# Issue counts in a front stage's plan, and the fourth rotation placed behind the memory's low parts

## The reference

```python
x = x + 0.5 * rms_norm(swiglu(rms_norm(x, g1), w_gate, w_up, w_down), g1_post)
h = rms_norm(x, mix_pre_g)
proj = h @ w_in                      # columns for attention and for the recurrence
o_nsa = nsa_mixer(q, k_cmp, v_cmp, k_slc, v_slc, k_win, v_win, gate_logits, ...)
o_rwkv = rwkv7_mixer(r, k, v, w_lo, a_lo, g_lo, ...)
x = x + rms_norm(concat([rms_norm(o_nsa), o_rwkv]) @ w_out)
x = x + rms_norm(memory_cross_attention(rms_norm(x), rms_norm(mem), wq, wk, wv, wo))
x = x + 0.5 * rms_norm(swiglu(rms_norm(x, g2), w_gate, w_up, w_down), g2_post)
```

## Time and profile before

| | |
|---|---|
| median of 3 runs | 2557.35 us (2555.98 to 2559.16) |
| the profiled execution | 2554.12 us, span 2552.3 us |
| TensorE busy | 2488.6 us, 98% of the span |
| TensorE in the stretches 1020 to 1030 and 1030 to 1040 | 9.01 and 8.64 of 10 us |
| end of the last product of the front stage, about | 1077.5 us |
| first instruction of the next stage | 1081.55 us |

### The profile page before, as it was taken

One profiled execution on the slowest core, in us unless ns is written; L12 is line 12 of the kernel. 1 busy time (PEld: TensorE's weight loads), 2 busy tenths in 40 slices (PEclk: granted clock), 3 DMA queues, 4 the chain that ended last, 5 costly groups with the idle time before them and its releaser, 6 DMA issues. The chain is left out here.

```text
span 2552.3 us, 47185 instructions
## 1 busy us (share of the span) xinstructions
PE 2488.6 (98%) x19392; PEld 2038.3 (80%) x19392; DVE 1711.0 (67%) x2707; ACT 1054.6 (41%) x1824; POOL 95.3 (4%) x146
## 2 busy tenths in 40 slices
PE   8999999999899999899999998999999999999998
PEld 7788888888787778877888886877777888888887
DVE  6876676687555354488878888534457866766676
ACT  4322323344533343456555565523343322323443
POOL 0000000000000000011231110000000000000000
PEclk9999999999999999989999999999999999999999
DMA  4323324655332268832212115411121423225464
GB/s 150 99 82 119 123 71 142 219 196 158 96 122 93 62 205 239 235 98 58 50 43 49 41 45 205 143 58 34 66 75 61 135 97 119 98 91 209 142 197 145
DMA packets 279269, 297.92 MB, mean 117 GB/s; under 512 B 75442, under 2 KB 209840, under 8 KB 279088
## 3 DMA queue, kind: packets, MB, share of 16 engines
q1 hardware_dynamic: 276208, 292.59, 36.1%
q10 hardware_dynamic: 2880, 2.75, 0.4%
HBM read 208.67 MB, written 81.36 MB: 114 GB/s over the span
## 5 line engine op out<-in xcount | busy, mean ns | idle before, releaser
L1141 PE MATMUL f_ps<-hi,f_wh 128*128 128x512 f32 x672 | 261.9, 390 | 4.1 <-DVE f_wl L847 4.1
L1143 PE MATMUL f_ps<-hi,f_wl 128*128 128x512 f32 x672 | 261.5, 389 | 0.0
L2630 PE MATMUL f_ps<-hi,f_ahead_h 128*128 128x512 f32 x392 | 163.2, 416 | 0.8 <-PEq L72 0.8
L2632 PE MATMUL f_ps<-hi,f_ahead_l 128*128 128x512 f32 x392 | 153.1, 390 | 0.0
L2631 PE MATMUL f_ps<-one_lo,f_ahead_h 128*128 128x512 f32 x392 | 152.9, 390 | 0.0
L1141 PE MATMUL f_ps<-f_t3h,f_t2h 128*128 128x512 f32 x392 | 152.5, 389 | 0.0
L1142 PE MATMUL f_ps<-f_t3l,f_t2h 128*128 128x512 f32 x392 | 152.5, 389 | 0.0
L1143 PE MATMUL f_ps<-f_t3h,f_t2l 128*128 128x512 f32 x392 | 152.5, 389 | 0.0
L1141 PEld LDWEIGHTS f_ps<-hi,f_wh 128*128 128x128 f32 x672 | 126.1, 188 | 31.4 <-DVE f_wl L847 4.9
L1143 PEld LDWEIGHTS f_ps<-hi,f_wl 128*128 128x128 f32 x672 | 126.1, 188 | 26.3
L1142 PE MATMUL f_ps<-one_lo,f_wh 128*128 128x512 f32 x352 | 137.0, 389 | 0.0
(11 more groups left out here) (592 smaller groups left out, 6602.0 us busy)
## 6 DMA issues: line engine op xcount, KB each, us to landing
act<-one_y SPq DMA_DIRECT2D x30, 512.0 KB, 3.5
f_work<-act SPq DMA_DIRECT2D x30, 512.0 KB, 3.6
act<-y SPq DMA_DIRECT2D x30, 512.0 KB, 3.5
arena<-act SPq DMA_DIRECT2D x30, 512.0 KB, 3.6
one_y<-in_w_in SPq DMA_DIRECT2D x25, 512.0 KB, 4.5
early<-in_ffn_w_gate SPq DMA_DIRECT2D x11, 1024.0 KB, 6.4
early<-in_ffn_w_up SPq DMA_DIRECT2D x11, 1024.0 KB, 8.9
f_raw<-in_ffn_w_gate SPq DMA_DIRECT2D x10, 1024.0 KB, 6.2
```

The source lines that it names most:

```text
L1141: nc.tensor.matmul(out, wh, xh, start=start, stop=False)
L1143: return nc.tensor.matmul(out, wl, xh, start=False, stop=stop)
L2630: nc.tensor.matmul(dense_ps[:, b, cols], w_hi[:, b, k, :], hi[:, k, cols], start=(k == 0), stop=False)
L2632: mm = nc.tensor.matmul(dense_ps[:, b, cols], w_lo[:, b, k, :], hi[:, k, cols], start=False, stop=(k == KD - 1))
```

## The change

It adds a constant `ISSUE`, 0.61 us for each transfer that SyncE issues, and uses it in the planned time of each of SyncE's events, multiplied by the number of transfers. It also gives rotation 3 (the fourth, counted from 0) a further need: the low part `mlo` 1 of the memory. No instruction is added or taken away; only the order can differ. The diff, cut to the lines that differ:

```diff
 HOP = 0.2
+ISSUE = 0.61
...
-        event(("load", c), "sp", 0.5, *free, c and ("load", c - 1))
+        event(("load", c), "sp", ISSUE * (1 + {1: 13, 3: 10, PROJECTED - 2: 11, PROJECTED: 11}.get(c, 0)), *free, c and ("load", c - 1))
...
-                event(("store_vm",), "sp", 0.2, ("vcopy", 1), late=4.0)
+                event(("store_vm",), "sp", ISSUE, ("vcopy", 1), late=4.0)
...
-        event(("store_ops", p), "sp", 0.6, ("res", p), late=6.0)
-        event(("store_gate", p), "sp", 0.2, ("gr", p, 1), late=4.0)
+        event(("store_ops", p), "sp", 4 * ISSUE, ("res", p), late=4.0)
+        event(("store_gate", p), "sp", ISSUE, ("gr", p, 1), late=4.0)
...
-        event(("store_bonus", p), "sp", 0.2, ("bfin", p), late=4.0)
+        event(("store_bonus", p), "sp", ISSUE, ("bfin", p), late=4.0)
...
-            event(("store_v", n), "sp", 0.2, ("tcopy", n), late=4.0)
-    event(("load_mem",), "sp", 0.5, ("store_ops", 3), ("store_bonus", 3), late=16.0)
+            event(("store_v", n), "sp", ISSUE, ("tcopy", n), late=4.0)
+    event(("load_mem",), "sp", 3 * ISSUE, ("store_ops", 3), ("store_bonus", 3), late=16.0)
...
-    event(("load_w1", 0), "sp", 0.2, ("load", 3), late=7.0)
-    event(("load_w1", 1), "sp", 0.2, ("hid", 0), late=14.0)
+    event(("load_w1", 0), "sp", ISSUE, ("load", 3), late=7.0)
+    event(("load_w1", 1), "sp", ISSUE, ("hid", 0), late=14.0)
...
-        event(("spread", s), "sp", 0.5, ("evac", MIXED + s), ...
+        event(("spread", s), "sp", 4 * ISSUE, ("evac", MIXED + s), ...
...
-        event(("store_c", s), "sp", 0.3, ("cfin", s), late=3.0)
-    event(("tables",), "sp", 0.3, ("res", 3), late=5.0)
+        event(("store_c", s), "sp", ISSUE * (2 - s), ("cfin", s), late=3.0)
+    event(("tables",), "sp", 2 * ISSUE, ("res", 3), late=5.0)
...
-        event(("swap", n), "sp", 0.5, ("evac", at[("rot", n)]), ...
-        event(("rot", n), "dve", 3.8, ("swap", n), ("tables",), n and ("rot", n - 1))
+        event(("swap", n), "sp", 4 * ISSUE, ("evac", at[("rot", n)]), ...
+        event(("rot", n), "dve", 3.8, ("swap", n), ("tables",), n and ("rot", n - 1), n == 3 and ("mlo", 1))
...
-        event(("store_rot", n), "sp", 0.3, ("rlo", n), late=5.0)
+        event(("store_rot", n), "sp", 2 * ISSUE, ("rlo", n), late=5.0)
```

More of the change, by code:

```diff
@@ L2316, in front_plan @@
         event(("mlo", t), "dve", 1.4, ("mhi", t), t and ("mlo", 0))
-    event(("load_w1", 0), "sp", 0.2, ("load", 3), late=7.0)
-    event(("load_w1", 1), "sp", 0.2, ("hid", 0), late=14.0)
+    event(("load_w1", 0), "sp", ISSUE, ("load", 3), late=7.0)
+    event(("load_w1", 1), "sp", ISSUE, ("hid", 0), late=14.0)
     for s in range(2):
-        event(("spread", s), "sp", 0.5, ("evac", MIXED + s), ("gather", 0) if s else ("store_ops", 2), s == 0 and ("res", 2), late=4.5)
+        event(("spread", s), "sp", 4 * ISSUE, ("evac", MIXED + s), ("gather", 0) if s else ("store_ops", 2), s == 0 and ("res", 2), late=4.5)
         event(("gather", s), "dve", 2.6, ("spread", s), *([("hid", 0)] if s else [("zw", 3), ("rate", 3, 1), ("g", 3, 1)]))
@@ L2325, in front_plan @@
         event(("cfin", s), "dve", 0.3 if s else 1.2, ("cout", s), s and ("cfin", 0))
-        event(("store_c", s), "sp", 0.3, ("cfin", s), late=3.0)
-    event(("tables",), "sp", 0.3, ("res", 3), late=5.0)
+        event(("store_c", s), "sp", ISSUE * (2 - s), ("cfin", s), late=3.0)
+    event(("tables",), "sp", 2 * ISSUE, ("res", 3), late=5.0)
     for n in range(6):
-        event(("swap", n), "sp", 0.5, ("evac", at[("rot", n)]), *([("rot", n - 2)] if n >= 2 else [("store_ops", 3), ("bsum", 3, 1)]), late=4.0)
-        event(("rot", n), "dve", 3.8, ("swap", n), ("tables",), n and ("rot", n - 1))
+        event(("swap", n), "sp", 4 * ISSUE, ("evac", at[("rot", n)]), *([("rot", n - 2)] if n >= 2 else [("store_ops", 3), ("bsum", 3, 1)]), late=4.0)
+        event(("rot", n), "dve", 3.8, ("swap", n), ("tables",), n and ("rot", n - 1), n == 3 and ("mlo", 1))
         event(("rhi", n), "act", 1.2, ("rot", n), n and ("rhi", n - 1), *([("store_rot", n - 2)] if n >= 2 else [("store_ops", 3), ("cum", 3, 1)]))
         event(("rlo", n), "dve", 1.3, ("rhi", n), *([("store_rot", n - 2)] if n >= 2 else [("bfin", 3), ("store_gate", 3)]))
-        event(("store_rot", n), "sp", 0.3, ("rlo", n), late=5.0)
+        event(("store_rot", n), "sp", 2 * ISSUE, ("rlo", n), late=5.0)
     return in_order(engine, takes, needs, lag)
```

## The result

The changed kernel takes 2562.99 us in the median of 20 runs (2558.52 to 2571.25), the one before 2556.88 us on the same chips (20 runs, 2554.51 to 2564.28). The ratio is 1.0023, with an interval of 1.0015 to 1.0030: 5.9 us slower, between 3.8 and 7.7. That is inside the range of the prediction, and just past the bound that parts "no difference" from "slower".

The account below looks back on a forecast made before the run. The prediction took TensorE, 98% busy, as the bound, with SyncE's chain from rotation 5 ending the front stage. Rotation 5's late stores delay SyncE's 30.6 us of issuing: plus 4.0 us, median 2561.4, range 2554.5 to 2565.5.

Parts of the forecast that it names:

- Order on VectorE behind slab 25: VectorE, late front stage: rotations 3 to 5 follow the memory's low parts, interleaved with splits; `rlo` 5 ends 4.4 us late.
- The counts cost nothing: Front stage ahead of 1020: new issue counts delay memory loads behind slab 23; cost nothing, at most 2 us.
- TensorE by itself 0.6 us late: TensorE, late front stage: 1.0 us wait won, new 1.8 us wait, 1.2 us replacing 1.4; net 0.6 us late.
- 1 us of wait more for slab 35: TensorE near the stage's end: slab 35 lands 4.0 us later, is wanted 0.6 later, against 2.4 us of slack.
- The store of rotation 5: SyncE's queue: rotation 5's second store is issued at 1045.3 instead of 1040.89.
- Landing: Rotation 5's second store, behind a bunch of transfers, takes 8.2 us to land, at 1053.5 against 1049.5.
- 30.6 us of pure issuing: SyncE from slab 35 to the stage's end: never idle, so the list keeps its length and ends 4.0 us later.
- From the stage's end to the total: Next stage: can't give lateness back, so a stage ending 4.0 us later makes the total 4.0 us longer.
- rival 3: Rotations pile up: ScalarE waits for rotation 3's stores, `rlo` 5 slips another 2.88 us; plus 6.9 us, 2564.3; chance 0.34.
- land alone: Rival: rotation 5's stores land in 3.6 us, SyncE restarts early; minus 0.6 to plus 0.5 us, 2557; chance 0.12.
- The win: Rival: TensorE loses both waits (2.4 us), SyncE's chain no later; 4 us won at most, 2553.4; chance 0.06.

Follow-up runs that it names:

- the counts alone: Changed kernel without rotation 3's need for the memory's low part 1, so only the issue counts differ from before: 2558.44 us, ratio 1.0002.
- the run with the need on rotation 4: Kernel before, with rotation 4 instead of rotation 3 made to need the memory's low part 1: 2557.77 us, ratio 1.0002.
- the two held kernels: Kernel before, with slab 35 also waiting for the low part of slab 33, or of slab 34: 2562.16 us and 2563.26 us.
- The repaired kernels: Changed kernel, slabs 35 and 36 released by rotations 4 and 5, later slabs by their own buffer's stores; timed twice: 2559.16 and 2560.25 us.
- transfers taken early in the changed kernel: Changed kernel, with the next stage's two operand groups "across" issued ahead of slab 35: 2559.74 us, ratio 1.0007.
- the need alone: Kernel before, with only rotation 3's need for the memory's low part 1 added: 2562.15 us, ratio 1.0023.
- before's order with the transfers taken early: Kernel before, with the next stage's two operand groups "across" issued ahead of slab 35: 2557.22 us, ratio 1.0002.

## Why the prediction was right, and where it was off

The sum was plus 4.0 us, and the largest chance (0.59) went to a change within the 5.1 us that can be told; it is slower by 5.9 us, a little more than that, for which the chance was 0.36. The mechanism is in the main the forecast one, the lateness of rotation 5 carried through two stores into SyncE's list. That a late slab 35 alone costs that much was shown by holding it; that it is all of the loss was not. By its steps:

- *Order on VectorE behind slab 25*: each of the thirteen places as worked out. `rlo` 5 was to be 4.4 us late, it is 4.3.
- *The counts cost nothing*: right in its result (ratio 1.0002), short in its reason. The loads of the memory do go behind slab 23 and its leads, as worked out, and rotation 2 is no later for it (it starts 37.0 us ahead of T0, before 36.4). But the plan also changes ahead of 1020 on ScalarE and VectorE, where I found nothing: the counts move some early activations ahead of high parts of weights, and `rot` 2 and a low part ahead of a normalization. TensorE is busy for all of 700 to 1000 in both kernels, and that covers it. By the plan, the counts alone also put rotation 4 behind the low parts; the run with the need on rotation 4 shows that this costs nothing that can be told.
- *TensorE by itself 0.6 us late* (1.0 won, waits of 1.8 and 1.2), and 1 us of wait more for slab 35: the waits for low parts are 1.5 and 0.9, together 2.4 as before, and that behind slab 35 is 0.3. ScalarE's last transfer is 0.8 us later against T0. It stays off the path, as forecast.
- *The store of rotation 5*: issued 24.9 us after T0, where the profile before had 19.35. That is 5.5 us late, and the forecast had 4.4. The missing 1.1 us is issuing itself: in the bunch the load ahead of it took 0.85 us and the first store 1.63, where a lone store takes 0.34 to 0.43. I had given the bunch a price for landing and none for issuing.
- *Landing*: 8.2 us forecast, 7.3 measured. The two errors, 1.1 us too little for issuing and 0.9 too much for landing, all but cancel, and slab 35 is 4.2 us late where 4.0 was said. That this term came out so close was luck. The size that the Trainium skill (DMA: Bandwidth & Descriptors, the section Anatomy of one DMA) would give, an estimated 3.2 us, is not seen for this store; the store stood behind five others.
- *"30.6 us of pure issuing"*: this is the step whose reasoning failed, though it cost the sum only 0.6 us. The list is not of fixed length: it took 31.2 us in the changed kernel, 32.2 and 32.0 with slab 35 held for 33 and 34, and 33.7 with it released early. The same six slabs took from 7.3 to 11.9 us to issue, so the transfers pace it at least in part. A slab 35 that comes 2.8 us later makes the end 4.4 us later; one that comes 2.8 us earlier leaves it where it was, and one 5.5 us earlier in before's order makes it 2.9 us earlier. Some of this is the spread of single executions: with the counts alone the list took 31.4 us, with slab 35 where it was before.
- *From the stage's end to the total*: taken as one to one. The profiles give +4.8 us at the stage's end, the times +5.9 (3.8 to 7.7). For the two held kernels it is +4.4 and +4.9, +7.0 and +8.2. These are a little above one to one, none by more than its interval. The repaired kernels don't fit: +0.5 and +2.8, and, clear of its interval, +0.3 and +4.6 (2.3 to 6.9). With the transfers taken early in the changed kernel it is +3.5 and +1.8.

So the forecast of 2561.4 was 1.6 us under the measured 2562.99. Against before it is 5.9 us where 4.0 was said. Of the 1.9 us between them 0.8 is the stage's end in the profile: 0.2 from the release of slab 35 and 0.6 from the list behind it. The other 1.1 us is within the interval. The median lies where the prediction had put rival 3 (above 2562.5), but not for rival 3's reason.

The rivals: the stores did not land alone (7.3 us, not 3.6). The pile-up did not come: ScalarE went from 1044.29 on with no wait for a store. The win could not come, for TensorE's 2.4 us of waits only changed their name.

What stays open: with the late release repaired, the changed order is still some 2 to 4 us above before, and its profiled executions don't show why. The counts alone show no loss (1.0002), though their interval reaches 4.3 us; whether the need and the split wait without the counts would show the same was not tried. So the late release is enough to make a loss of this size, as the held kernels show, but it isn't shown to be all of it in the changed kernel; taken back, it returns 1.3 and 3.1 of the 5.9 us by the two timings.

## What to carry to other kernels

Before moving a step into the busy part of an engine's order, ask what its last successor releases on the queues; here VectorE had idle time at 1009 for a rotation, and the cost of not using it appeared some 70 us later, as a late start of the next stage on an engine that had nothing to do with it. A chain of issues that looks like pure issuing can be held by its transfers, and behind it another engine may be nearly as late: here a later slab 35 cost its lateness and more, and an earlier one paid in part or not at all. And if two waits stand in a row on the bound engine, removing the first is worth nothing until the work behind the second is earlier too.

## What the hardware showed that was not expected

TensorE's granted clock falls at the change of stage, 2.8 us behind the last product before and 3.7 us behind it after (in the waits of 4.2 and 8.1 us), and stays at half for a while after the engine works again. Stretches of before, then of after (length; busy of PE, PEld, DVE, ACT, POOL; clock; DMA share; GB/s):

```profile
1080.00:1085.00 5.00, 2.15 (x34) 1.87 (x34) 0.00 (x0) 0.00 (x0) 0.95 (x4) 0.54 1.09 364
...
1095.00:1100.00 5.00, 4.64 (x101) 3.98 (x102) 4.76 (x24) 2.51 (x9) 3.17 (x7) 0.50 0.02 3
1100.00:1105.00 5.00, 5.00 (x124) 4.44 (x124) 4.14 (x26) 3.72 (x14) 1.86 (x3) 0.92 0.18 41
```

```profile
1085.00:1090.00 5.00, 0.92 (x10) 0.83 (x14) 0.00 (x0) 0.00 (x0) 0.95 (x4) 0.50 1.20 258
...
1105.00:1110.00 5.00, 4.78 (x93) 4.29 (x92) 4.85 (x15) 1.99 (x6) 4.03 (x6) 0.50 0.07 17
1110.00:1115.00 5.00, 5.00 (x126) 4.29 (x121) 2.32 (x19) 3.53 (x14) 0.00 (x0) 0.81 0.33 74
```

The lower level (0.50, 1.2 GHz) lasts until 1100.8 before and until 1111.9 after, 19.3 and 23.0 us past the start of the stage. Over all the profiles this is 19 to 25 us, and in the one of the counts alone it was 49 us; that execution's span was 2566.6 us although its kernel's median is 2558.44. The third line of the table follows it: 473.1 us where the lower level lasted 19.3 us into the stage (before and the need alone), 474.8 to 475.2 for 23.0 to 23.8, 476.0 for 24.9 and 484.4 for 49. It doesn't follow the length of TensorE's wait: the need alone has a wait of 8.3 us and the shortest stretch. One such stretch can hide or feign a difference of 10 us, so a single profile of this kernel decides nothing about its total.

A second dip, of 0.83 for the stretch 690 to 700, came in six of the fourteen profiled executions (that of the changed kernel, and also that of before's order with the transfers taken early) and not in the others (the need alone, the counts alone: 1.00). It goes with a T0 of 1023.7 or later, where the others have 1021.5 to 1022.9, so it costs some 2 us. It belongs to the execution and not to the change. A third dip near 1980, in eight of the fourteen, does the same to the last line of the table: 998.7 to 1000.0 us with it, 997.0 to 998.1 without. The changed kernel's profile has it and that of before doesn't:

```profile
1975.00:1995.00 20.00, 17.94 (x72) 14.37 (x71) 17.60 (x16) 6.84 (x7) 0.00 (x0) 0.91 0.40 127
```

So the three lines of the table in which the change doesn't act, 6.8 of the 11.6 us, go in the main with the granted clock of the two executions that happened to be profiled.
